# Late modulation products moved out of a state recurrence into the passages between stages, and feed-forward tiles put into two ring slots

## The reference

```python
def adaln_params(c, w, b):
    mod = jax.nn.silu(c) @ w + b
    shift, scale, gate = jnp.split(mod, 3, axis=-1)

def modulate(x, g, shift, scale):
    return rmsnorm(x, g) * (1.0 + scale) + shift

def second_block(...):
    h = x
    for i in range(2):
        shift, scale, gate = adaln_params(c, ada_w[i, 0], ada_b[i, 0])
        hn = modulate(h, norm_g[i, 0], shift, scale)
        m = s5_mixer(hn, ...) if i % 2 == 0 else fox_mixer(hn, ...)
        h = h + gate * m
        shift, scale, gate = adaln_params(c, ada_w[i, 1], ada_b[i, 1])
        hn = modulate(h, norm_g[i, 1], shift, scale)
        h = h + gate * conv_ffn(hn, ffn_w_up[i], conv_w[i], conv_b[i], ffn_w_down[i])
    return rmsnorm(h, final_g)
```

## Time and profile before

| | |
|---|---|
| median of 3 runs | 1424.56 us (1424.35 to 1435.64) |
| the profiled execution | 1422.76 us, span 1421.0 us |
| PE, DVE, ACT busy | 1237.4, 706.8, 457.5 us |
| mean granted clock of TensorE | 0.900 of full speed |
| HBM read | 369.94 MB |
| the chain that ended last | PE 61%, DMA 23%, DVE 8%, POOL 3%, ACT 3% |

### The profile page before, as it was taken

One profiled execution on the slowest core, in us unless ns is written; L12 is line 12 of the kernel. 1 busy time (PEld: TensorE's weight loads), 2 busy tenths in 40 slices (PEclk: granted clock), 3 DMA queues, 4 the chain that ended last, 5 costly groups with the idle time before them and its releaser, 6 DMA issues.

```text
span 1421.0 us, 21785 instructions
## 1 busy us (share of the span) xinstructions
PE 1237.4 (87%) x8798; PEld 904.4 (64%) x8798; DVE 706.8 (50%) x1109; ACT 457.5 (32%) x650; POOL 179.3 (13%) x273
## 2 busy tenths in 40 slices
PE   5989888787788787788798979999979888899997
PEld 4758654432333333334765969999959676899995
DVE  6467741122111221212467647776754674676776
ACT  5244232111111111111534435444433531544432
POOL 1000257423032030320021000000000000000000
PEclk9989979888888889878899989999979968899998
DMA  6871598999999999999497234445425501355441
GB/s 238 338 291 60 213 388 348 428 428 428 429 428 428 428 428 429 428 428 428 165 408 284 90 134 178 177 177 182 171 105 186 200 1 74 118 209 190 177 177 45
DMA packets 36607, 371.73 MB, mean 262 GB/s; under 512 B 4149, under 2 KB 5710, under 8 KB 12622
## 3 DMA queue, kind: packets, MB, share of 16 engines
q1 hardware_dynamic: 33984, 364.66, 63.3%
q10 hardware_dynamic: 2574, 6.38, 1.3%
HBM read 369.94 MB, written 1.08 MB: 261 GB/s over the span
## 4 chain that ended last, share of the span: by engine, by line
PE 61%; DMA 23%; DVE 8%; POOL 3%; ACT 3%; issue 2%; ACTq 0%; DVEq 0%; POOLq 0%
PE ps L651 58%; DMA ring<-in_w_up 22%; PE ps L671 1%; DMA ring<-in_ada_w 1%; ACT ring_parts L473 1%; PE ps L896 1%; DVE W L1961 1%; DVE W_parts L1777 0%; DVE XH L1745 0%; DVE X L2176 0%; ACT XH L1243 0%; DVE XH L1932 0%; DVE XH L2175 0%; DVE W_parts L2266 0%; DVE ring_parts L481 0%
## 5 line engine op out<-in xcount | busy, mean ns | idle before, releaser
L651 PE MATMUL ps<-W_parts 128*128 128x256 f32 (+1 forms) x2736 | 412.7, 313 | 15.3 <-DVE W_parts L1777 6.5
L651 PEld LDWEIGHTS ps<-W_parts 128*128 128x128 f32 x2736 | 377.9, 196 | 47.6 <-issue 20.3
L651 PE MATMUL ps<-ring,W 128*32 128x512 f32 x1536 | 221.4, 725 | 73.0 <-DMA ring<-in_w_up 42.6
L651 PEld LDWEIGHTS ps<-ring,W 128*32 128x32 f32 x1536 | 52.1, 127 | 221.8 <-issue 154.3
L651 PE MATMUL ps<-W 128*32 128x64 f32 (+8 forms) x1664 | 154.0, 300 | 18.2 <-DVE W L2148 7.3
L651 PEld LDWEIGHTS ps<-W 128*128 128x128 f32 (+4 forms) x1664 | 106.3, 169 | 70.9 <-issue 51.8
L2266 DVE TENSOR_TENSOR W_parts<-ring,W_parts 128x2048 fp32r<-128x2048 f32 x44 | 100.9, 2293 | 29.7 <-ACT W_parts L1505 29.7
L2144 DVE COPY W<-ps 128x1024 f32<-128x1024 f32 x16 | 19.6, 1224 | 175.7 <-PE ps L651 175.7
L651 PE MATMUL ps<-XH_parts,ring_parts 128*128 128x256 f32 x512 | 95.2, 289 | 5.1 <-issue 5.0
L651 PE MATMUL ps<-ring_parts,W_parts 128*128 128x512 f32 (+1 forms) x304 | 91.2, 402 | 3.2 <-issue 3.2
L651 PEld LDWEIGHTS ps<-kc,W 128*128 128x128 f32 x640 | 85.6, 218 | 12.6 <-issue 6.3
(11 more groups left out here) (350 smaller groups left out, 1313.2 us busy)
## 6 DMA issues: line engine op xcount, KB each, us to landing
ring<-in_w_gate SPq DMA_DIRECT2D x32, 2048.0 KB, 21.8
ring<-in_w_up SPq DMA_DIRECT2D x32, 2048.0 KB, 26.6
ring<-in_w_down SPq DMA_DIRECT2D x32, 2048.0 KB, 23.2
ring<-in_ada_w SPq DMA_DIRECT2D x24, 2048.0 KB, 12.1
ring<-in_up SPq DMA_DIRECT2D x44, 1024.0 KB, 5.5
ring<-in_dn SPq DMA_DIRECT2D x44, 512.0 KB, 3.3
ring<-in_fox_in SPq DMA_DIRECT2D x6, 2048.0 KB, 7.7
ring<-in_w_in SPq DMA_DIRECT2D x4, 1024.0 KB, 13.0
```

The lines of the kernel that those rows point to most:

```text
L651: return pe.matmul(o, l, r, start=a, stop=z_, skip_group_check=True, **kw)
```

## The change

The late products are moved out of the recurrence, in four groups of three (`LATE`). The group 12 to 14 stands at the passage before s5: two products before the turn and one behind it; the group's own turn (`ada_turn`) comes between the two halves of the s5 input product. The group 15 to 17 is placed in the same way at the passage to feed-forward 0, the group 18 to 20 at the passage to fox. Of the group 21 to 23, two products stand in the attention of fox behind the first scores, and one behind the turn that follows the attention. A modulation of layer 2 or 3 is finished half by half.

For that the ring's plan is rewritten: up and down tiles of a feed-forward share a slot (columns 0 to 2047 and 2048 to 3071), two slots for both, so that four slots are free for modulation and fox blocks. The zero matmuls of `ffn` stand behind the first up product. Some semaphores are merged.

```diff
     load("s5", 2, apart=True, to=4)
-    load("ada", 8, to=2)
-    load("s5", 1, apart=True, to=4)
-    load("ada", 2, to=0)
...
-    load("up1", 2, NF // 2, to=0)
-    load("down1", 2, NF // 2, to=4)
+    load("ada", 2, to=2)
+    load("ada", 1, to=2)
+    for first in (2, 4, 0, 2):
+        load("s5", 1, apart=True, to=first)
+    load("ada", 2, to=4)
+    load("up0", 2, NF // 2, to=0)
+    load("ada", 1, to=4)
+    load("fox", 1, apart=True, to=2)
+    load("ada", 1, to=5)
+    load("ada", 1, to=4)
+    order.append(("tiles", 0))
+    load("fox", 1, apart=True, to=0)
+    load("ada", 1, to=5)
+    for first in (4, 2, 0, 4):
+        load("fox", 1, apart=True, to=first)
+    load("ada", 2, to=2)
+    load("fox", 1, apart=True, to=0)
+    load("ada", 1, to=2)
     load("fox", 1, apart=True, to=4)
+    load("up1", 2, NF // 2, to=2)
+    order.append(("tiles", 1))
...
-ADA_AT = [((2 * c,), (2 * c + 1,)) for c in range(6)] + [((12,), ()), ((), ())]
+LATE = {12: (12, 15), 15: (15, 18), 18: (18, 21), 21: (21, 24)}
...
+            ada_product(12)
+            ada_product(13)
             turn(3)
+            ada_product(14)
             first_ready(3)
-            for i in range(2):
-                features("s5", i, XNr, s5l, (4 + 2 * i, 5 + 2 * i), "u_mm", turned=None if i else 3)
+            features("s5", 0, XNr, s5l, (4, 5), "u_mm", turned=3)
+            ada_turn(2, 0)
+            features("s5", 1, XNr, s5l, (6, 7), "u_mm")
...
             def ffn(k, turned):
+                if k == 0:
+                    pe.wait_ge(S("bank4_read"), 1)
+                    ada_product(15, 4)
+                    ada_product(16, 4)
                 turn(turned)
-                for b in range(4, 8):
-                    mm(ps[:, b, :], zb[0:1, 0:P], zb[0:1, :], True, False)
+                if k == 0:
+                    ada_product(17, 4)
...
                 up(0, 0, True)
+                if k == 0:
+                    ada_turn(3, 1)
+                for b in range(4, 8):
+                    mm(ps[:, b, :], zb[0:1, 0:P], zb[0:1, :], True, False)
                 gate_rows(2 * k + 1, (2, 3))
...
+            def two_products():
+                ada_product(21)
+                ada_product(22)
-            attention(8, lambda s: None)
+            attention(8, lambda s: None, two_products)
             turn(6)
+            ada_product(23)
```

More of the change, by code:

```diff
@@ L589, in ffn_tiles @@
                 for b in range(2):
[L590 to L599, removed]
+                    s = begin(f"up{k}", b) if first else slot_of[f"up{k}", b]
+                    if not first:
+                        sp.wait_ge(S("up_low"), i * 2 + (NF * k + b - 1))
+                    sp.dma_start(ring[:, s, 0:2048], (up0, up1)[k][ds(i * 2 + b, 1)].rearrange("a p n -> p (a n)")
+                                 ).then_inc(filled_sem[s], 16)
+                    if not first:
+                        sp.wait_ge(S("down_low"), i * 2 + (NF * k + b - 1))
+                    sp.dma_start(ring[:, s, 2048:3072], (dn0, dn1)[k][ds(i * 2 + b, 1)].rearrange("a p n -> p (a n)")
+                                 ).then_inc(S(f"down{b}_filled"), 16)
             for name, i in order:
@@ L624, in _ @@
                     load(begin(name, i), SLOT, block((s5_in, s5_glu, s5_out)[i // 2], i % 2))
[L625 to L628, removed]
                 elif name == "fox":
                     load(begin(name, i), SLOT, block(fox_in, i) if i < 6 else block(fox_out, i - 6))
-                elif name == "up1" and i == 0:
-                    ffn_tiles(1, 0, True)
+                elif name in ("up0", "up1") and i == 0:
+                    ffn_tiles(int(name[-1]), 0, True)
+                elif name == "tiles":
                     with sp.Fori(1, NF // 2) as i2:
-                        ffn_tiles(1, i2, False)
+                        ffn_tiles(i, i2, False)
             for t in range(NT):
@@ L921, in outputs, with attention @@
                 last.then_inc(S("pv_mm"), 1)
-            def attention(first, between):
+            def attention(first, between, opened=None):
                 scores(first)
                 scores(first + 1)
+                if opened:
+                    opened()
                 for s in range(first, first + 8):
@@ L1187, in _ @@
                 features("fox", i, XNr, foxl, (2 * i, 2 * i + 1), "fox_mm", turned=None if i else 5)
-            for i in range(2):
-                features("fox", 2 + i, XNr, foxl, (4 + 2 * i, 5 + 2 * i), "fox_mm")
+            ada_turn(4, 7)
+            features("fox", 2, XNr, foxl, (4, 5), "fox_mm")
+            pe.wait_ge(S("ada_kept"), 5)
+            features("fox", 3, XNr, foxl, (6, 7), "fox_mm")
             pe.wait_ge(S("fk_copied"), 1)
@@ L1202, in _ @@
                                     K("ident")[0:FH, 0:FH])
-            last.then_inc(S("F_turned"), 1)
+            last.then_inc(S("f_mm"), 1)
             gate_rows(2, (6, 7))
@@ L1555, in _ @@
                     apart_high(act, 8 + j // 2)
+            ada_keep(4, 18, 21)
             apart_high(act, 10)
@@ L2186, in _ @@
             features_in(3, lambda c: gsc[:, 0, c:c + 1], lambda c: mod[:, 0, c:c + 1], (XNr, s5l), (0, 1))
-            for half in range(2):
-                apart_low(v, 1, half)
+            for n in (1, 2):
+                for half in range(2):
+                    apart_low(v, n, half)
             def turns(ct):
@@ L2239, in _ @@
                     ready = driven(ct + 1)
-            modulation(LAYERS, 1, LAYERS)
             y_low(1)
@@ L2281, in ffn @@
                 down_low(0, 0)
+                if k == 0:
+                    modulation(4, 2, 3)
                 cw, cb = COLS["convw"][0], COLS["convb"][0]
@@ L2361, in _ @@
             features_in(6, None, None, (oh, foxl))
+            modulation(6, 3, 4)
             v.wait_ge(S("gate_copied"), 3)
```

140 lines of the change are left out of this document (66 added, 74 removed).

## The result

The changed kernel takes 1436.53 us (median of 4 runs, 1436.23 to 1448.7); the kernel before, run beside it, takes 1424.45 (4 runs, 1423.81 to 1435.64). The medians differ by 12.1 us (0.85%); the ratio on record is 1.012, with a 95% interval of 1.008 to 1.016, so 12 to 23 us. The change makes the kernel slower. The forecast was 1426 and no change. The time lies outside the 1420 to 1432 that the forecast gave for its two cancelling terms, and inside the wider 1414 to 1439 that allowed for rivals. The profiled executions, 1422.76 before and 1436.32 after, differ by 13.5 us in their spans, and what follows takes that sum apart.

A forecast was written before the change was run, and what follows sets the result against it. PE was taken to bound the recurrence only through its products, DVE without them. Terms -21 + 1.9 + 1.0 + 2.5 + 1 + 15 + 1 + 1 = +2.4 us on 1422.8 gave 1425.2, taken as 1426; range 1420 to 1432.

The forecast's parts named there:

- two cancelling terms: Recurrence -21 us against ACT's wait in fox's attention +15 us, cancelling within a few microseconds; chance 0.65, range 1420 to 1432.
- rivals: Clock falls in recurrence, 0.15; passages late, about 1434, 0.10; ACT's wait hidden, 1411, 0.08; recurrence faster than DVE's pace, 0.02.
- The large term on ACT: Fox's attention: ACT waits for the last fox weight block, so its first exponential comes 15 us later, 14 to 17.
- its closing section: Signs expected in the trace after, among them ACT idle some 15 us and SP issuing ada_w and fox_out at about 1117.
- The passage to fox: Before fox's input product: products 18 to 20 and the group's turn cost +2.5 us, between +1 and +5.
- feed-forward 0: First feed-forward with the passage ahead: +1.0 us, between -0.6 and +4; second pair's first tile lands at about 856.
- 8 x 5.43 = 43.4 us of DVE: Recurrence: eight groups at DVE's first-group pace, the main part of a stretch cut from 69.47 us, -21 us.
- the 0.6 for ACT: Recurrence: 0.6 us added to 47.9 for ACT making whole 3.6 us high parts between two small copies.
- the lower clock: Rival in the recurrence: PE at the lower clock throughout costs +13 us, 1439; half the time 1432; 0.15 for 5 us or more.
- the passage before s5: Products 12 to 14 around the turn before s5's input product: +1.0 us, and +0.95 for the group's turn, together +1.9.
- the forget sums: Two loads of 2 MB more run when the forget sums are written and spread: +1 us, bounds 0 and 3.
- the zero matmuls, the last turn, product 23: Behind fox's attention: product 23 and the group's turn +1 us; four zero matmuls in PE's path, second feed-forward, +1 us.

## Why the forecast was wrong

**Right.** The large term on ACT was right in mechanism and size: 15.7 us of idle time ahead of the high part, released by fox_out, with SP issuing ada_w at 1130.76 and fox_out at 1131.18, and the landing 12.11 us later against the 11.6 worked out. The forecast had the scores' end at 1129.67 as in the trace of before; it was 1128.8. So its closing section, which expected these two issues at about 1117, was off by 14 us: of the 14.6 us that it held saved by then, only 0.8 were. The wait's length doesn't depend on that, since everything in it is counted from the scores. The passage to fox (+2.8 for 2.5) was right with its parts: the turn took 1.94 us where it took 3.65 before, and product 20 waited 4.17 us for its block. So was feed-forward 0: the second pair of tiles came late by about 2 us (ACT waits 2.48 us for it), inside the bounds of that step. That modulation's last products keep the clock up in the passages is shown by the turns (1.97, 1.94, 1.94 us).

**Wrong: "8 x 5.43 = 43.4 us of DVE".** The 5.43 came from the one group in which POOL does nothing, and it was taken for all eight. The trace of before had the stretched instructions in plain sight, in its second and third group, with POOL's product beside each:

```profile
723.85 2.09 DVE L2221 TENSOR_TENSOR_SCAN XH<-W,XH 128x256 f32<-128x256 f32 x2
...
732.79 2.06 DVE L2227 TENSOR_TENSOR W<-XH,W 128x512 f32<-128x512 f32 x2
```

```profile
724.25 1.15 POOL L1728 TENSOR_TENSOR W<-W,kc 128x512 f32<-128x512 f32 x1 [1.97 <-PE ps L651]
...
732.63 1.07 POOL L1728 TENSOR_TENSOR W<-W,kc 128x512 f32<-128x512 f32 x1 [4.10 <-PE ps L651]
```

In the first group of that trace the scans take 1.27 us and L2227 1.29. A group with POOL's product costs about 6.28. This is 4.3 of the 6.6 us missed in the recurrence (2.9 are the clock, and the 0.6 for ACT was not needed).

**Undersized: the clock.** The forecast put the lower clock in a rival, at 0.15 for 5 us or more, and nothing in its own sum, with the words "these matmuls leave no gap above 1 us". That took PE's idle time as spread over the group. PE's timeline shows it in one piece, gaps of 2.21, 1.96 and 2.14 us where the clock is full, since PE waits for the states of a group and then has everything to do at once. The clock fell in the first of these gaps, soon after the second, and not at the third, and cost 2.9 us. The section of the Trainium skill that the forecast cited on short idle times between groups of matmuls ("TensorE: Matmul & The Clock Gate", "A second HAM failure mode: psum-queue depth-cycling") was right that the clock goes up and down; what it costs here is 2.9 us, not the 13 of the rival.

**Undersized: the passage before s5, with its block 13 in at 682.** The landings were read from one execution of the kernel before. They belong to a stream of loads that runs at full rate through the experts: block 12 lands 507 to 508 us after the first of the experts' loads is issued, in the trace of before (169.26, about 677, one block ahead of the stream's end at 682) as in the changed kernel's (173.85, 681.0) and in one that started it at 178.57 (686.0). The start of that stream differs by up to 9 us from one execution to the next, by what goes on in the first attention, which the change leaves alone. (The first attention has a granted clock of 1.00 from 150 to 170 us in the trace of before, and of 0.78 in the other trace of that kernel, whose stream starts at 174.26.) In the kernel before it hardly matters: with that start, in the run with the one ACT copy moved, s5's input product began at 688.77 against 688.06. In the changed kernel PE waits for blocks 12, 13 and 14 in turn, which land 5 and 6 us apart, so it is the landing of the third, 691.9, and its product that s5 waits for. The forecast reckoned with the landing of block 13 and with none for block 14. SP's row for the three shows what holds the third:

```profile
669.16 15.52 SPq L578 DMA_DIRECT2D ring<-in_ada_w  x3
```

Block 14 goes to the slot of block 12, so SP can issue it only when product 12 is done, at 684.36, and it lands 7.5 us later. That is the same shape as the wait in the attention: a load behind a product in one slot. The step was forecast at +1.9 and measured +4.3. An estimate of how much of this is the stream: were it to start where it did in before's trace, 4.6 us earlier, and all landings with it, the term would be about nothing; no run shows that. So a part of the 13.5 us between the two profiled executions is the moment at which the stream starts, to which the changed kernel is exposed and the kernel before is not.

**Mis-sized: the forget sums, "+1; bounds 0 and 3".** The write of 16 KB took 5.1 instead of 1.5 us, 3.6 us more, and the wait of PE behind it (2.55 us) let the clock fall, so the matmuls after it took 0.63 instead of 0.40 us until 1117. It was 4.3 in all. The forecast priced "two loads of 2 MB more" and did not ask where in their transfer the write would come: with some 1.7 MB of it still to come (5.1 us at the 341 GB/s of the window).

**Too dear: the zero matmuls, the last turn, product 23**, forecast at +2 behind the attention, -0.8 measured. The clock is higher there (0.90 instead of 0.86 between the turn behind the attention and feed-forward 1), which may be what pays for them; no run takes them out one by one.

All misses but the last point one way. The forecast took its durations from stretches without the neighbour (POOL's products, the end of the experts' stream, two loads under way) that the same work has in the changed kernel.

## What to carry to other kernels

When work that hid an engine's pace is taken away, take that pace from a stretch in which all its neighbours also run, and look for the same instruction at two durations in the trace of before: the longer one is what a neighbour costs. When a product is moved to just behind a full stream of loads, its block lands at the stream's end, and one that shares a slot with an earlier product a whole load after that product. And when a program issues loads in a fixed order, put the slow copy that waits for the last of them behind the work that doesn't need it: one moved ACT instruction turned this change from a ratio of 1.012 to one of 0.996, and with one moved load to 0.991.

## What the runs showed that was not expected

- A DVE instruction on 128x256 with both inputs in SBUF took 0.42 us alone and 1.28 us beside a POOL product of 128x512, and one that reads PSUM kept its 0.68 us; without POOL's six products DVE's busy time in the recurrence fell by 4.25 us.
- The granted clock fell from 1.00 to 0.50 in an idle time of PE of 2.2 us, stayed there for 12 us of nearly full work (PE 7.77 of 8 us busy) in one execution, and fell later and for 3 to 4 us at a time in another of the same code; a matmul of 1.12 us at the start of each gap kept it at 1.00 throughout.
- A write of 16 KB took 5.1 us behind two loads of 2 MB, and 1.4 us without them, although another engine issued it.
- Products of 2 us put ahead of an attention that PE did not fill lifted its mean clock from 0.67 to 0.88 and made it 4.2 us shorter; without them the same attention had 0.64 and was not shorter.
